# A transformer block with attention, feed-forward and experts: the identity products in TensorE's waits are taken out at the second feed-forward norm and in the router

## The chip, the cores and the metric

The kernel runs on one core of one Trainium2 chip. Its time is the device time of the launch in microseconds, the median of several runs. The engines are named as the profile names them: PE is TensorE's matmul, PEld its weight load, DVE is VectorE, ACT ScalarE, POOL GpSimd, SP SyncE, and a q behind a name is that engine's queue.

## The reference

The reference takes 256 tokens of 1024 features through three layers. All is float32. Cut to the calls that matter:

```python
def second_block(x, c, ...):
    for i in range(2):
        ...
        h = _modulate(x, sh_a, sc_a)          # rms norm, then * (1 + scale) + shift
        m = _neighborhood_attention(...) if i == 0 else _mla(...)
        x = x + g_a[:, None, :] * m
        h = _modulate(x, sh_f, sc_f)          # i == 0: the second feed-forward norm
        f = _swiglu(...) if i == 0 else _moe(h, w_router, w_gu, w_down)
        x = x + g_f[:, None, :] * f
    return _rmsnorm(x) * final_norm

def _moe(h, w_router, w_gu, w_down):
    ...
    probs = softmax(hf @ w_router)            # 8 experts
    vals, idx = lax.top_k(probs, 2)
    ...
    for e in range(8):
        y = y + combine[:, e:e + 1] * _swiglu(hf, w_gu[e], w_down[e])
```

Ahead of it, first_block is a layer of its own: norm, causal attention beside a recurrent unit, output projection, norm, feed-forward. So there are six norms that feed a projection, numbered 0 to 5 in the kernel: 0 and 1 in the first block, 2 and 3 in the first layer of the second, 4 and 5 in its last, where 5 is the one of the router.

## The kernel before

The 256 tokens stand in two row tiles of 128 (t = 0, 1), the features in eight column tiles of 128 (k). Weights come from HBM by SyncE's DMA queue into a ring of raw buffers. Most are split into a rounded high part (ScalarE, whi) and the rest (VectorE, wlo), and a product is then made of three: high by high, low by high, high by low. A raw buffer is loaded again when both parts are made, and the parts are made again when TensorE has used them. Each engine runs its own list in the order in which it is written, and semaphores tie them together.

The norm of stage s (whole_pair, L870, called by whole_columns) runs as follows. The output projection ahead of it ends row tile 0 first. VectorE multiplies it by its gate and adds it to x (L2172, L2173), ScalarE sums the squares (L1424), VectorE scales the rows by the reciprocal root (L1903). TensorE transposes the eight column tiles (L837) into PSUM, and ScalarE (k below 4, L1438) and VectorE (the others, L1908) modulate them into hx; for row tile 1 the two engines change sides. VectorE's list has the residual add of row tile 1 between the norm of row tile 0 and its modulation of it. TensorE multiplies two raw weight blocks by each tile of hx (whole_side, L859), turns row tile 1 in the middle of it, and ends with whole_rest (L867). In the stage of the second feed-forward norm (s = 3) the function fill makes two products of the 128x128 identity with 512 constant columns into a PSUM bank that is not used at that time, ahead of the first transposes. They end in no result.

The router (stage 5) works on both row tiles. TensorE transposes row tile 0 of x inside the last output projection (router_begin), makes its logits (L1267, eight columns), transposes row tile 1 (turn_rows, by halves as VectorE adds them up at L2375), and makes its logits. ScalarE copies the transposes (L1777), VectorE copies the last half (L2377). ScalarE sums the squares of row tile 1 behind its first copy. VectorE reads the logits (L2383), ranks them (L2395 to L2402) and names the two chosen experts of each token; five small products (L1281 to L1285) count places and totals; VectorE makes from the places the matrix that picks the rows of expert 0 (L2414), splits a weight block (L1893), and TensorE gathers these rows turned (L1299). VectorE modulates the first half of them (L2424), then works out from the totals which expert runs in which pass (L2442 to L2454, into eidi). SyncE, ScalarE and GpSimd wait for that list (sem experts_known); SyncE has by then filled all its buffers with the first weights of expert 0, and goes on with the next ones after it. The passes of the experts follow (expert_pass, L1341 and L1368). fill is called at five places in the router: one product after the logits of row tile 0, one after the transposes of row tile 1, two ahead of the wait for the chosen experts, one after the five small products, one after the gather.

Of the kernel before, what the change touches and what calls it, by code (L numbers as in the profile page):

```python
# [300 lines left out]
def blocks(nc, a, out):  # L301

    ctx = ExitStack()
    with ctx:
        base = [(nc.sbuf_base + LINE - 1) // LINE * LINE]

        def at(name, cols, dt=F32, offset=None, parts=P):

            if offset is None:
                offset = base[0]  # L310
                base[0] += (cols * 4 + LINE - 1) // LINE * LINE
                assert base[0] <= nc.sbuf_usable_end, (name, base[0], nc.sbuf_usable_end)
            t = nc.alloc_sbuf_tensor_at(name, [parts, cols], dt, offset=offset)
            return t.ap() if hasattr(t, "ap") and callable(t.ap) else t[:, :]
# [9 lines left out]
        def sem(name):  # L324
            if name not in sems:
                sems[name] = ctx.enter_context(nc.semaphore(name))
            return sems[name]
# [30 lines left out]
        cst = at("cst", C_ALL)  # L358
# [121 lines left out]
        ps = ctx.enter_context(nc.psum_tensor("ps", [P, 8, 512], F32))  # L480

        ident = cst[:, C_ID:C_ID + P]
# [12 lines left out]
        def vec(name):  # L495
            _, _, n, col = VEC[name]
            return vecs[:, col:col + n]
# [279 lines left out]
        def _(pe):  # L777
# [46 lines left out]
                        between()  # L824
                m.then_inc(mm_done, 2)

            def fill(bank, count):

                for _ in range(count):
                    pe.matmul(ps[:, bank, :], ident, cst[:, 0:512], start=True, stop=True)  # L830

            def turn_rows(rows_, s, t, by_half=None):

                for k in range(KT):
                    if by_half and k % 4 == 0:
                        pe.wait_ge(by_half, k // 4 + 1)
                    m = pe.transpose(ps[:, TURN_BANK[s] + 2 * t + k // 4, k % 4 * P:(k % 4 + 1) * P],  # L837
                                     rows_[:, t, k * P:(k + 1) * P], ident)
                    if k in (3, KT - 1):
                        m.then_inc(sem("turned"), 1)  # L840

            def turn(s, t):

                pe.wait_ge(sem("xn_ready"), XN0[s] + t + 1)
                turn_rows(xn, s, t)

            def whole_raw(c, width):

                ck = Chunk(c)
                pe.wait_ge(raw_in[ck.slot], 16 * ck.loads)  # L850
                return view(raws[ck.slot], KT, width)

            def whole_side(parts, t, s):

                for k in range(KT):
                    e, count = mods_until(s, t, k)
                    pe.wait_ge(mods_done[e], count)
                    for w, (o, cols) in parts:
                        pe.matmul(o[:, t * P:(t + 1) * P], w[:, k, cols], hx[:, t, k], start=(k == 0), stop=(k == KT - 1))  # L859
# [9 lines left out]

            def whole_pair(first, s, widths, pieces, after_turn=None, before_turn=None):  # L870

                fill(2, {1: 0, 3: 2}.get(s, 0))
                turn(s, 0)
                if after_turn:
                    after_turn()
                w = [whole_raw(first + i, widths[i]) for i in range(2)]
                whole_side([(w[i], pieces[i][0]) for i in range(2)], 0, s)
                if before_turn:
                    before_turn()
                turn(s, 1)  # L880
                for i in (1, 0):
                    whole_side([(w[i], pieces[i][1])], 0, s)
                return w
# [5 lines left out]
            def whole_columns(first, s, banks, after_turn=None):  # L889

                pieces = two_tiles(banks)
                w = whole_pair(first, s, (256, 256), pieces, after_turn)
                for i in range(2):
                    whole_rest(w[i], pieces[i], s)
# [297 lines left out]
            kv = [(ps[:, 5, 0:S], slice(0, KVL)), (ps[0:ROPE, 0, 0:S], slice(KVL, KVL + ROPE))]  # L1192
            queries = [(ps[:, 4, f * S:(f + 1) * S], slice(f * P, (f + 1) * P)) for f in range(2)]
            wd = whole_pair(W_MDN, 4, (KVL + ROPE, QL), (kv, queries), None, lambda: pe.wait_ge(sem("mod_read1"), 2))
            whole_rest(wd[0], kv, 4)
            latent_sum(0, (2,))
# [18 lines left out]
            for t in range(NT):  # L1215
                pe.wait_ge(sem("keys_read"), t + 1)
                tok = slice(t * P, (t + 1) * P)
                for lhs, rhs in ((lat_hi, h), (lat_hi, l), (lat_lo, h)):
                    for n in range(2):
                        m = pe.matmul(ps[:, 2 * t + n, :], lhs[:, 2, tok], rhs[:, n * 512:(n + 1) * 512],  # L1220
                                      start=(lhs is lat_hi and rhs is h), stop=(lhs is lat_lo))
# [36 lines left out]
            def logits(t):  # L1258

                for k in range(KT):  # L1260
                    if (t, k) == (1, 4):
                        pe.wait_ge(sem("x_half"), 3)
                    elif k % 4 == 0:
                        pe.wait_ge(sem("aT_ready"), AT0[5] + 2 * t + k // 4 + 1)
                    if (t, k) == (0, 0):
                        pe.wait_ge(sem("shift_read"), 1)
                    m = pe.matmul(ps[:, 4 + t, 0:NE], xT[:, t, k], rscaled[:, k], start=(k == 0), stop=(k == KT - 1))  # L1267
                m.then_inc(sem("logits"), 1)

            output_projection(W_MLO, KT, *mixes[3], 4, begun=2, last=(HEADS0[3] + H2) // 2, inside=router_begin)  # L1270
            logits(0)
            fill(0, 1)
            turn_rows(x, 5, 1, sem("x_half"))
            fill(0, 1)
            logits(1)

            fill(3, 2)
            pe.wait_ge(sem("chosen"), 1)
            sel = rw[:, 8:10, :].rearrange("p t e -> p (t e)")
            tri = cst[:, C_TRI:C_TRI + P]  # L1280
# [2 lines left out]
            pe.matmul(ps[:, 5, NE:2 * NE], ones, sel[:, 0:NE], start=False, stop=True).then_inc(sem("places"), 1)  # L1283
            pe.matmul(ps[:, 4, 0:NE], ones, sel[:, 0:NE], start=True, stop=False)
            pe.matmul(ps[:, 4, 0:NE], ones, sel[:, NE:2 * NE], start=False, stop=True).then_inc(sem("totals"), 1)  # L1285
            fill(3, 1)

            def begin_expert(c, p):
                ck = ExpertChunk(c, p, PASS_CHUNKS)
# [3 lines left out]
            def gather_turned():  # L1293

                pe.wait_ge(sem("pick_ready"), 1)
                pe.wait_ge(sem("xn_ready"), XN0[5] + NT)
                for k in range(KT):
                    for t in range(NT):
                        m = pe.matmul(ps[:, 6 + k // 4, k % 4 * P:(k % 4 + 1) * P], xn[:, t, k * P:(k + 1) * P],  # L1299
                                      pick[:, t, :].bitcast(F32), start=(t == 0), stop=(t == NT - 1))  # L1300
                    if k == 3:
                        m.then_inc(sem("gathered_first"), 1)
                m.then_inc(sem("gathered_turned"), 1)
# [12 lines left out]
                m.then_inc(sem("ge_turned"), 1)  # L1316

            gather_turned()
            fill(0, 1)

            def expert_pass(p, last):

# [62 lines left out]
            for n in range(2):  # L1385
                pe.wait_ge(sem("last_ready"), n + 1)
                for t in range(NT):
                    for d in (dchi, dclo):
                        m = pe.matmul(ps[:, 6 * (1 - t) + n, :], pickT[:, t * P:(t + 1) * P], d[:, n * 512:(n + 1) * 512],
                                      start=(d is dchi), stop=(d is dclo))  # L1390
# [5 lines left out]
        def _(act):  # L1396
# [79 lines left out]
            for name, (tile, row, count, _) in VEC.items():  # L1476
                if name not in SP_ROWS:
                    ld(rows[row:row + count, tile, :], VEC_SRC[name](a), "rows_in")
# [1219 lines left out]
```

## Time and profile before

| | |
|---|---|
| time, median of three runs | 1258.85 us |
| the three runs | 1258.27, 1258.85, 1261.66 us |
| span of the profiled execution (the page gives no other time of it) | 1258.0 us |
| TensorE busy | 1224.1 us, 97% of the span |
| VectorE busy | 1016.2 us, 81% |
| ScalarE busy | 779.0 us, 62% |
| TensorE's mean granted clock | 0.996 of full speed |
| HBM read and written | 375.4 MB, 298 GB/s over the span |

The span is that of one execution under the profiler, and all positions and durations below are from it. A busy TensorE is not one at its peak: the page counts an instruction as busy from its start to its modelled end, and neighbouring matmuls overlap. So the duration of a group is read off the chain of waits, where each piece ends where the next begins. A float32 product stands in the trace as two instructions, a transpose and a product of the rounded parts as one.

### The profile page before, as it was taken

How to read it: one execution, taken by the hardware profiler on the slowest of the kernel's cores; microseconds unless marked ns; L12 is line 12 of the kernel's file. 1: busy time of each engine (PE TensorE's matmuls, PEld its weight loads, DVE VectorE, ACT ScalarE, POOL GpSimd, SP SyncE). 2: the span in 40 equal slices, each digit the busy share in tenths (PEclk: the TensorE clock that was granted, in tenths of full speed). 3: DMA queues.
4: the chain of work that ended last, by engine and by line, in shares of the span. 5: the costliest groups of instructions: out<-in, count | busy, mean ns of one | idle time of the engine just before them, and what ended most of it. 6: DMA issues, size and time to landing. Idle time of an engine off the chain costs nothing.

```text
span 1258.0 us, 20244 instructions
## 1 busy us (share of the span) xinstructions
PE 1224.1 (97%) x7668; PEld 1086.8 (86%) x7668; DVE 1016.2 (81%) x1095; ACT 779.0 (62%) x992; POOL 93.1 (7%) x111
## 2 busy tenths in 40 slices
PE   9989999999999999999999999999999999999995
PEld 7978999987998799998897777898989898989884
DVE  6797899996756588777756578989898989898987
ACT  5765666644655455443346556777777777777764
POOL 0020000000562100000002202000000000000020
PEclk9999999999999999999999999999999999999998
DMA  9953997679944569998973239999999999999991
GB/s 322 377 200 102 337 314 270 246 289 252 250 159 162 181 215 325 332 349 308 382 253 97 79 140 394 379 406 355 401 351 409 348 408 349 408 345 411 347 410 73
DMA packets 163981, 369.08 MB, mean 293 GB/s; under 512 B 24420, under 2 KB 96559, under 8 KB 157511
## 3 DMA queue, kind: packets, MB, share of 16 engines
q1 hardware_dynamic: 157345, 350.72, 78.0%
q10 hardware_dynamic: 5094, 12.11, 2.5%
q0 software_dynamic: 1472, 5.28, 1.1%
q8 instruction: 49, 0.80, 0.3%
q14 instruction: 21, 0.17, 0.0%
HBM read 360.72 MB, written 14.70 MB: 298 GB/s over the span
## 4 chain that ended last, share of the span: by engine, by line
PE 71%; DVE 12%; ACT 4%; issue 4%; DMA 3%; SPq 3%; POOL 2%; ACTq 0%; DVEq 0%
PE ps L1341 20%; PE ps L795 7%; PE ps L797 7%; PE ps L796 7%; PE ps L1368 6%; PE ps L807 4%; PE ps L809 4%; PE ps L811 4%; DVE wlo L1893 3%; SPq L712 2%; PE ps L859 2%; PE ps L867 2%; DMA raw<-in_moe_w_gu 2%; DVE third_lo L1893 2%; DVE wlo L1885 1%
## 5 line engine op out<-in xcount | busy, mean ns | idle before, releaser
L1406 ACT ACTIVATE whi<-raw 128x1024 fp32r<-128x1024 f32 x186 | 192.6, 1057 | 152.0 <-PE ps L797 96.1
L1885 DVE TENSOR_TENSOR wlo<-raw,whi 128x1024 fp32r<-128x1024 f32 x186 | 227.1, 1248 | 72.8 <-ACT whi L1406 69.3
L795 PE MATMUL ps<-ahi,whi 128*128 128x256 f32 x832 | 234.3, 282 | 0.3 <-ACT qT L1591 0.3
L796 PE MATMUL ps<-alo,whi 128*128 128x256 f32 x832 | 231.8, 279 | 0.0
L797 PE MATMUL ps<-ahi,wlo 128*128 128x256 f32 x832 | 231.8, 279 | 0.0
L1893 DVE TENSOR_TENSOR wlo<-raw,whi 128x1792 fp32r<-128x1792 f32 (+1 forms) x96 | 199.3, 2089 | 24.4 <-ACT whi L1420 24.3
L1420 ACT ACTIVATE whi<-raw 128x1792 fp32r<-128x1792 f32 (+1 forms) x96 | 167.5, 1758 | 55.9 <-PE ps L1368 24.0
L795 PEld LDWEIGHTS ps<-ahi,whi 128*128 128x128 f32 x832 | 156.9, 189 | 1.7 <-issue 0.8
L796 PEld LDWEIGHTS ps<-alo,whi 128*128 128x128 f32 x832 | 156.7, 188 | 0.7 <-issue 0.7
L797 PEld LDWEIGHTS ps<-ahi,wlo 128*128 128x128 f32 x832 | 156.9, 189 | 0.0
L1341 PE MATMUL ps<-whi,hchi 128*128 128x448 f32 x352 | 101.8, 370 | 4.0 <-DVE wlo L1893 2.7
L1341 PE MATMUL ps<-wlo,hchi 128*128 128x448 f32 x352 | 99.1, 362 | 0.0
L1341 PE MATMUL ps<-whi,hclo 128*128 128x448 f32 x352 | 99.0, 362 | 0.0
L1341 PEld LDWEIGHTS ps<-whi,hchi 128*128 128x128 f32 x352 | 63.8, 187 | 16.5 <-DVE wlo L1893 6.7
L1893 DVE TENSOR_TENSOR third_lo<-raw,third_hi 128x1792 fp32r<-128x1792 f32 (+1 forms) x32 | 66.8, 2088 | 10.8 <-ACT third_hi L1420 10.7
L1420 ACT ACTIVATE third_hi<-ada 128x1792 fp32r<-128x1792 f32 (+2 forms) x32 | 51.2, 1601 | 31.4 <-PE ps L1341 18.9
L1341 PEld LDWEIGHTS ps<-wlo,hchi 128*128 128x128 f32 x352 | 66.0, 188 | 4.5
L1341 PEld LDWEIGHTS ps<-whi,hclo 128*128 128x128 f32 x352 | 66.0, 188 | 4.6
L1893 DVE TENSOR_TENSOR third_lo<-ada,third_hi 128x1792 fp32r<-128x1792 f32 (+2 forms) x32 | 60.3, 1886 | 7.4 <-ACT third_hi L1420 7.4
L1893 DVE TENSOR_TENSOR wlo<-ada,whi 128x1792 fp32r<-128x1792 f32 (+2 forms) x32 | 60.4, 1887 | 4.5 <-ACT whi L1420 4.3
L2611 POOL TENSOR_SCALAR probs<-probs,small 128x256 f32<-128x256 f32 (+1 forms) x80 | 48.7, 623 | 187.0 <-DVE small L2025 186.7
L1420 ACT ACTIVATE whi<-ada 128x1792 fp32r<-128x1792 f32 (+2 forms) x32 | 51.0, 1595 | 17.4 <-PE ps L1341 16.0
(350 smaller groups left out, 2431.7 us busy)
## 6 DMA issues: line engine op xcount, KB each, us to landing
raw<-in_moe_w_gu SPq DMA_DIRECT2D x96, 896.0 KB, 7.0
ada<-in_w_ada SPq DMA_DIRECT2D x48, 1024.0 KB, 7.4
raw<-in_moe_w_down SPq DMA_DIRECT2D x32, 1024.0 KB, 7.9
ada<-in_moe_w_gu SPq DMA_DIRECT2D x32, 896.0 KB, 7.3
raw<-in_w_up SPq DMA_DIRECT2D x22, 1024.0 KB, 5.8
raw<-in_ffn_w_gu SPq DMA_DIRECT2D x22, 1024.0 KB, 9.1
ada<-in_moe_w_down SPq DMA_DIRECT2D x16, 1024.0 KB, 9.2
raw<-in_na_w_qkv SPq DMA_DIRECT2D x12, 1024.0 KB, 8.4
```

What stands on the lines that cost most here:

```text
L795: pe.matmul(o, h[:, k, cols], bhi[:, k], start=(k == 0), stop=False)
L796: pe.matmul(o, h[:, k, cols], blo[:, k], start=False, stop=False)
L797: m = pe.matmul(o, l[:, k, cols], bhi[:, k], start=False, stop=(k == KT - 1))
L807: pe.matmul(o, bhi[at_k][:, tok], h[:, k, n0:n0 + n], start=first, stop=False)
L809: pe.matmul(o, bhi[at_k][:, tok], l[:, k, n0:n0 + n], start=False, stop=False)
L811: m = pe.matmul(o, blo[at_k][:, tok], h[:, k, n0:n0 + n], start=False, stop=last)
L1341: m = pe.matmul(ps[:, 2 * part + n, 0:EC], lhs[:, kk], rhs[:, k, n * EC:(n + 1) * EC], start=(kk == 0 and lhs is hchi and rhs is h), stop= ...
L1368: m = pe.matmul(ps[:, 4 + n, :], lhs[:, k0 + k], rhs[:, k, n * 512:(n + 1) * 512], start=(k0 + k == 0 and rhs is h and lhs is gchi), stop= ...
L1406: act.activation(high_, src, ACT.Copy).then_inc(hi_done, 1)
L1420: act.activation(high_[:, 0:k * n], raws[ck.slot][:, 0:k * n], ACT.Copy).then_inc(moe_hi, 1)
L1885: ve.tensor_tensor(low_, src, high_.bitcast(F32), ALU.subtract).then_inc(lo_done, 1)
L1893: ve.tensor_tensor(low_[:, 0:k * n], raws[ck.slot][:, 0:k * n], high_[:, 0:k * n].bitcast(F32), ALU.subtract)\
```

## The change

Every call of fill goes, and the function with them. Nothing is put in their place, and no semaphore changes.

```diff
-            def fill(bank, count):
-
-                for _ in range(count):
-                    pe.matmul(ps[:, bank, :], ident, cst[:, 0:512], start=True, stop=True)
-
...
             def whole_pair(first, s, widths, pieces, after_turn=None, before_turn=None):
 
-                fill(2, {1: 0, 3: 2}.get(s, 0))
                 turn(s, 0)
...
             logits(0)
-            fill(0, 1)
             turn_rows(x, 5, 1, sem("x_half"))
-            fill(0, 1)
             logits(1)
 
-            fill(3, 2)
             pe.wait_ge(sem("chosen"), 1)
...
             pe.matmul(ps[:, 4, 0:NE], ones, sel[:, NE:2 * NE], start=False, stop=True).then_inc(sem("totals"), 1)
-            fill(3, 1)
...
             gather_turned()
-            fill(0, 1)
```

## Rows read from the trace of the kernel before

**Rows 1.** Waits of TensorE, 445 to 735 us: total, times, longest (us).
```profile
PE ps L984 <- DVE alo L2030: 0.3, 1, 0.3
```

**Rows 2.** Timeline of SyncE's queue: start, length, DMA issues of a line.
```profile
748.69 5.77 SPq L644 DMA_DIRECT2D raw<-in_moe_w_gu  x4
```

**Rows 3.** Windows: length, busy time of each engine (count), PEclk, DMA share, GB/s.
```profile
59.00:62.00 3.00, 3.00 (x28) 3.00 (x27) 1.97 (x6) 3.00 (x10) 0.00 (x0) 1.00 0.99 404
66.50:69.50 3.00, 3.00 (x16) 3.00 (x15) 3.00 (x3) 2.98 (x5) 0.00 (x0) 0.50 0.02 5
309.50:310.70 1.20, 0.10 (x2) 0.08 (x1) 0.47 (x2) 1.17 (x5) 0.00 (x0) 1.00 0.90 132
...
745.60:746.80 1.20, 0.00 (x0) 0.00 (x0) 1.03 (x7) 1.17 (x4) 0.00 (x0) 1.00 0.00 0
...
770.00:780.00 10.00, 8.77 (x43) 7.47 (x41) 6.88 (x5) 4.40 (x3) 0.00 (x0) 1.00 1.03 415
```

**Rows 4.** Chain of waits at the second feed-forward norm: start, length (us).
```profile
440.11 1.72 PE ps L830 x4
...
442.90 3.81 PE ps L859 x32
446.71 0.87 PE ps L837 x8
```

**Rows 5.** Timeline of VectorE and ScalarE at the same norm.
```profile
441.41 1.23 DVE L2173 TENSOR_TENSOR x<-x,xn 128x1024 f32<-128x1024 f32 x1
442.30 1.51 ACT L1438 ACTIVATE hx<-ps,mod 128x128 f32<-128x128 f32 x4 [3.71 <-PE ps L837]
442.74 1.37 DVE L1908 TENSOR_SCALAR hx<-ps,mod 128x128 f32<-128x128 f32 x4
443.69 1.07 ACT L1424 ACTIVATE xn<-x 128x1024 f32<-128x1024 f32 x1
445.40 0.76 DVE L1903 TENSOR_SCALAR xn<-x,small 128x1024 f32<-128x1024 f32 x1
```

**Rows 6.** Chain of waits in the router.
```profile
730.75 1.68 PE ps L1267 x16
732.44 0.96 PE ps L830 x2
...
733.87 0.60 ACT xT L1777
734.47 1.05 ACT xn L1424 x2
...
736.74 0.36 DVE rw L2383 x2
...
738.93 0.39 PE ps L1281 x2
...
740.21 0.96 PE ps L830 x2
741.17 1.80 PE ps L1299 x16
```

**Rows 7.** Timeline of VectorE and TensorE in the router.
```profile
731.52 0.69 DVE L2375 TENSOR_TENSOR x<-x,xn 128x512 f32<-128x512 f32 x1
...
732.85 0.69 DVE L2375 TENSOR_TENSOR x<-x,xn 128x512 f32<-128x512 f32 x1
...
734.31 0.69 DVE L2377 COPY xT<-ps 128x512 f32<-128x512 f32 x1 [0.77 <-PE ps L837]
...
736.67 1.96 PE L830 MATMUL ps<-cst 128*128 128x512 f32 x4
...
740.29 0.48 DVE L2414 TENSOR_SCALAR pick<-cst,posn 128x128 fp32r<-128x128 f32 x2
740.69 2.02 DVE L1893 TENSOR_TENSOR wlo<-raw,whi 128x1792 fp32r<-128x1792 f32 x1
```

**Rows 8.** Timeline of TensorE ahead of the fall of its clock.
```profile
65.96 0.78 PE L998 MATMUL ps<-cst,probs 128*128 128x128 f32 x3 [1.55 <-POOL probs L2611]
```

## The prediction

> **What bounds the kernel now.** I read TensorE's own waits first, then SyncE and the windows behind the router, then the chain of waits and the timeline around each place where the change cuts, and at last the windows that give the granted clock. Between the second feed-forward norm and the router TensorE hardly waits: the longest wait there is 0.3 us [rows 1]. A microsecond won on TensorE at the norm is therefore a microsecond won until the router. In the router the chain changes engine with every step (TensorE, ScalarE, VectorE and back), so there a product counts only where the next step waits for it. After the router the chain passes from VectorE's list of experts to SyncE, which takes up the expert weights again at 748.69 [rows 2]; from then on the DMA engines are full, a share of 1.03 and 415 GB/s between 770 and 780 us [rows 3]. What moves that list moves the end.
>
> **What is taken out.** Each call of fill makes products of the identity with 512 columns; a product is two instructions in the trace. Four instructions are 1.72 us on the chain [rows 4], so one product is 0.86 us. Eight products go: two ahead of the norm's first transposes, six in the router. The call for the first feed-forward norm had count 0, so nothing changes there. No wait and no transfer is added or moved, and no other engine loses an instruction.
>
> **The norm: 1.45 us earlier.** The two products are on the chain from 440.11 to 441.83, and the transposes of the first row tile follow them [rows 4]. That tile has long been ready, so without them the transposes start at 440.11. Not all of the 1.72 us stays, because VectorE becomes late. The eight modulated tiles are shared: ScalarE makes the first four, VectorE the last four, and VectorE starts its four only after the residual add of the second row tile, 441.41 + 1.23 = 442.64 [rows 5]. It starts them at 442.74 with or without the products. TensorE reaches the fifth tile after half of its 3.81 us [rows 4]: 442.90 - 1.72 + 1.9 = 443.08. The tile is there at 442.74 + 1.37/4 = 443.08 and a hand-over later, so at most 0.1 to 0.2 us is lost. More is lost at the second transposes. They need the second normalised row tile, ready at 445.40 + 0.76 = 446.16 now [rows 5]. Its squares on ScalarE (443.69) wait today behind ScalarE's own four tiles; without the products those (1.51 us from 440.11 + 0.47 on, [rows 5]) are done by 442.1, and the squares start when x is complete, at about 442.72. That is 0.97 us earlier, so the row tile is ready at 445.19 and the transposes start at about 445.25 instead of 446.71 [rows 4]: 1.46 us. I take 1.45. Bounds: 1.72 if VectorE's hand-overs were free, 0 if something after it does not move.
>
> **The router: 1.05 us earlier at full clock.** (a) The product ahead of the second transposes and the one after them. The product stands at 732.44 to 733.40 on the chain [rows 6]. The first half of x is there at 731.52 + 0.69 = 732.21 [rows 7], so the four transposes of it move 0.96 us forward, ScalarE's copy of them (0.60 us, now at 733.87) ends at about 733.5, and the squares of the second row tile, now at 734.47, wait instead for x itself, 732.85 + 0.69 = 733.54 [rows 6, 7]. They gain 0.8 to 0.9 us; I take 0.8. The other branch, the logits, must arrive as early: last transposes at 733.56 plus 0.45, VectorE's copy 0.69 (today it begins at 734.31, [rows 7]), then eight instructions of 1.68/16 = 0.105 us [rows 6], about 735.6. Now VectorE reads the logits at 736.74 [rows 6]; minus 0.8 that is 735.94, so the logits are not late. (b) The two products at 736.67, 1.7 us on the chain's measure, run while VectorE ranks the logits; TensorE's next real product starts at 738.93 on VectorE's result [rows 6, 7]. They cost nothing now and gain nothing. (c) The product at 740.21 keeps the gather until 741.17 [rows 6], though the pick matrix is there at 740.29 + 0.48 = 740.77 [rows 7]: 0.4 us less a start of 0.1 to 0.15, so 0.25. What is late next is VectorE's 2.02 us split at 740.69 [rows 7], which stands ahead of its reading of the gather: moved by 0.8 it ends at 741.9, and the first half of the gather (1.80 us, [rows 6]) ends at 739.97 + 0.06 + 1.80 = 741.85 instead of 742.97. So 0.8 + 0.25 = 1.05 us. (d) The last product lies before a wait: TensorE does nothing from 745.6 to 746.8 [rows 3]. Gain nothing. Together with the norm, 2.5 us.
>
> **What the products covered: the clock.** The trace has one place where the granted clock fell in mid-kernel. TensorE stood idle for 1.55 us before 65.96, after a few short attention products [rows 8]; from 66.50 to 69.50 the rows show 0.50, the 1.2 GHz level, and TensorE got through 16 instructions where it had got through 28 in the 3 us from 59 to 62 [rows 3]: a factor of 1.75. At the third norm, 1.1 us of idle in 309.50 to 310.70 left the clock at 1.00 [rows 3]. At the norm that is changed the new idle pieces are 0.2 and 0.35 us, shorter than the one that left the clock alone, so I cost it at nothing there. In the router it is another matter. After the change TensorE ends the logits at about 735.6, stands until 738.1, runs ten instructions of 8 columns (738.93 to 740.21 today, [rows 6]), stands until 740.0 and then gathers: over 4 us with 1.28 us of light work, thinner than what stood ahead of the fall at 66. I take a fall there as likely. Its price by the rows: three microseconds at half clock do the work of 3/1.75 = 1.7, so 1.3 us if all of it is on the path. If it starts at 738.1 it slows the six rank products ahead of the pick (0.77 us by 0.58) and the first part of the gather by some 0.3, together 0.9; if it starts in the pause before the gather it takes 1.3. I take 1.2; bounds 0 and, for a stretch twice as long, 2.6. Sum: -1.45 - 1.05 + 1.2 = -1.3 us.
>
> The Trainium skill, in "TensorE: Matmul & The Clock Gate", section "Part 1: The HAM clock gate", has it that half rate is the default and that activity lifts it. By that rule the fillers buy speed and the sum is -1.3; by the row at 309.50 they buy nothing and the sum is -2.5.
>
> **The rivals.** One: the clock holds in the router, as it held at 309.50 [rows 3]. Against it stands the thin work from 735.6 to 740.0. Time: -2.5 us. Two, on the other side: the clock stays low from the second tile's logits through the gather and the experts' first products. Place: TensorE, 734 to 750 us. Price at 0.75 of the time of each step on the path: last transposes and logits (0.45 + 0.84) 0.95, rank products 0.58, first half of the gather 1.35, and up to 1.3 for the first expert products; together 4.2, so +1.7 us. It turns the sign from 2.5 us on; the first three make 2.9 by themselves. For it: the logits have 8 columns an instruction, and the last cover, before 746.8, goes as well. Against it: the logits' weight loads keep TensorE going, and delays of the first expert products lie beside a DMA stream that is full [rows 3]. The Trainium skill, in "TensorE: Matmul & The Clock Gate", section "HAM oscillation — how this bites in real kernels", describes such a case, short bursts between waits that start at half rate each time; no stretch of this trace shows it twice in a row. Three: the norm's gain does not reach the end, because a weight load or a split keeps its time. Against it: TensorE waits for nothing over 0.3 us until 735 [rows 1], and loads are issued when splits free their buffers, so they move along. Time: -1.05 + 1.2 = +0.15 us.
>
> **How the numbers follow.** The profiled span is 1258.0 us, 0.85 below the median of the three runs, 1258.85; the page gives no other time of that execution. The differences are carried to the median. Forecast (one fall): 1258.85 - 1.3 = 1257.55, chance 0.5. No fall: 1256.35, 0.2. Low clock throughout: 1260.55, 0.17. Gain lost at the norm: 1259.0, 0.13. The runs of one kernel lie 0.6 below to 2.8 above their median, which is more than some of these differences; I go from 0.75 below the second case to 0.75 above the third: 1255.6 to 1261.2. A measurement of this kernel can tell about 0.3%, 3.8 us, from no change; none of the four cases reaches that, and only a sum of a case with the spread of the runs does: faster 0.06, same 0.84, slower 0.10.
>
> **What would show it.** Right: the transposes of the norm follow the projection at once, and TensorE's first modulated product runs some 1.7 us, the second transposes 1.45 us earlier than now, relative to the end of the projection; the rank products start 0.8 us earlier relative to the first logits; the granted clock is below 1.00 somewhere in the 10 us around the gather; SyncE takes up the expert weights about 1.3 us earlier in all. Wrong: a granted clock under 1.00 at the norm, a clock of 1.00 all through the router, a new wait of TensorE between norm and router, or an expert pass whose length changes from its period now.

## The result, and the profile after

The changed kernel took 1264.03 us (median of four runs, 1263.14 to 1265.63) beside 1259.59 us of the kernel before in the same measurement: a ratio of 1.0039, 95% interval [1.0025, 1.0053]. It is slower by 0.39%, where the prediction said 1257.6 us and no measurable change. Later measurements of the same two kernels came out smaller, 1.0013 [0.9995, 1.0032] and 1.0027 [1.0013, 1.0041]. Over everything measured the mean of the changed kernel is 1263.17 us (28 runs) and that of the kernel before 1260.33 us (190 runs): 2.84 us more, plus or minus 0.96 (95%), or 0.22%. One run of the kernel before, 2037.76 us at a mean granted clock of 0.556, was in a slow state and is left out. The loss is real; the first measurement probably shows it too large. The measurements behind the first ran on three chips, and the mean of the kernel before lay between 1259.7 and 1261.3 us in them, so comparisons across measurements are less sharp than their intervals say.

The head of the page of the changed kernel:

```profile
span 1261.3 us, 20212 instructions
PE 1220.9 (97%) x7652; PEld 1088.0 (86%) x7652; DVE 1018.7 (81%) x1095; ACT 778.8 (62%) x992; POOL 90.5 (7%) x111
```

TensorE is busy for less time than before (1220.9 us, 1224.1 before) and the span is 3.3 us longer. Cut into stages by rows of the timeline, the two profiled executions differ so:

| stage | before | after | difference |
|---|---|---|---|
| start, to the last product of the projection ahead of the norm | 439.48 | 442.42 | +2.9 |
| norm: from there to the second transposes | 7.07 | 5.71 | -1.36 |
| from there to the last product of the last projection | 283.58 | 283.59 | 0.0 |
| router: from there to the list of experts | 16.44 | 18.70 | +2.26 |
| from the list to the end | 511.43 | 510.88 | -0.55 |

So 0.9 us of the 3.3 arose where the change was made. The 2.9 us lie ahead of any edit, and a section below tells what they are.

**The norm went as worked out.** The chain of waits in the changed kernel, at the norm (start, length, what; a line of the code has another number in each kernel, so the transposes are L837 before and L832 here):

```profile
442.58 0.48 PE ps L811 x2
...
443.09 1.24 DVE xn L2161
...
444.35 1.24 DVE x L2162
...
447.32 0.77 DVE xn L1892
...
448.13 1.09 PE ps L832 x8
449.22 3.57 PE ps L854 x32
```

The chain leaves TensorE at the end of the projection and runs over VectorE's residual add (444.35) and second row tile (447.32) to the second transposes at 448.13. Before, it ran over the products and TensorE's own work [rows 4]. VectorE has become the bound, which is why 1.36 of the 1.72 us stay.

**The router lost its clock.** The chain there:

```profile
735.84 2.67 PE ps L1261 x16
738.53 0.24 DVE rw L2372
...
740.60 0.60 PE ps L1272 x2
741.20 0.43 PE ps L1273 x2
...
743.12 3.69 PE ps L1289 x16
746.84 1.37 DVE hc L2413 x4
```

The logits of the second tile (L1261) took 2.67 us; before, the chain ran over those of the first tile, the same sixteen instructions, in 1.68. The first two instructions of the rank products (the five small ones that count places and totals; L1272, 0.60) took 0.39, and the first half of the gather (L1289, 3.69) took 1.80 [rows 6]. On TensorE's timeline the gather began at 741.01 in the kernel before:

```profile
741.01 3.73 PE L1299 MATMUL ps<-pick,xn 128*128 128x128 f32 x32
```

so up to 742.97, where its first half ended on the chain, it took 1.96 us; the chain counts 1.80 because the gather overlaps the product ahead of it. Windows of the changed kernel (length, busy time of PE, PEld, DVE, ACT, POOL with counts, PEclk, DMA share, GB/s):

```profile
735.50:736.00 0.50, 0.50 (x8) 0.50 (x5) 0.12 (x1) 0.50 (x1) 0.00 (x0) 1.00 0.00 0
736.00:736.50 0.50, 0.50 (x6) 0.50 (x5) 0.50 (x1) 0.47 (x3) 0.00 (x0) 0.83 0.00 0
...
740.00:743.00 3.00, 2.30 (x10) 2.21 (x10) 1.24 (x8) 0.03 (x1) 0.00 (x0) 0.50 0.00 0
743.00:746.50 3.50, 3.38 (x16) 3.38 (x17) 2.00 (x2) 0.00 (x0) 0.00 (x0) 0.50 0.00 0
...
746.50:747.00 0.50, 0.50 (x6) 0.50 (x6) 0.16 (x1) 0.00 (x0) 0.00 (x0) 0.93 0.00 0
```

TensorE's timeline shows where the logits lie, and the wait behind them in brackets:

```profile
735.68 2.82 PE L1261 MATMUL ps<-rscaled,xT 128*128 128x8 f32 x16
740.60 0.60 PE L1272 MATMUL ps<-rw,cst 128*128 128x8 f32 x2 [2.10 <-DVE rw L2391]
```

The granted clock falls to 0.50 within the logits (736.0 to 736.5) and comes back at about 746.5, within the gather: 10.2 us at the 1.2 GHz level. The kernel before had 1.00 throughout this stretch. SyncE takes up the expert weights at 752.54, where it did at 748.69 [rows 2]:

```profile
752.54 5.76 SPq L644 DMA_DIRECT2D raw<-in_moe_w_gu  x4
```

Of these 3.85 us, 2.9 are from the start, -1.36 from the norm, 2.26 from the router.

This is not a matter of one trace. The granted clock as a mean over a whole run is 0.990 to 0.993 in all 28 runs of the changed kernel. In the 186 runs of the kernel before whose clock is on record it is 0.993 to 0.998, and 0.993 in only three of them.

### The profile page after: what moved, and what is told of

It is laid out like the page before. It is cut to its first block, busy times and chain, and to the rows that moved or that the text cites. A ratio compares the mean times of both kernels' runs of the same rounds, so it can differ in the third digit from the quotient of the medians.

```text
span 1261.3 us, 20212 instructions
## 1 busy us (share of the span) xinstructions
PE 1220.9 (97%) x7652; PEld 1088.0 (86%) x7652; DVE 1018.7 (81%) x1095; ACT 778.8 (62%) x992; POOL 90.5 (7%) x111
## 4 chain that ended last, share of the span: by engine, by line
PE 78%; DVE 11%; ACT 4%; issue 4%; DMA 1%; POOL 1%; ACTq 0%; DVEq 0%; SPq 0%
PE ps L1330 22%; PE ps L797 7%; PE ps L796 7%; PE ps L795 7%; PE ps L1357 6%; PE ps L807 5%; PE ps L809 5%; PE ps L811 5%; PE ps L862 3%; DVE wlo L1882 3%; PE ps L854 2%; DVE third_lo L1882 2%; DVE wlo L1874 1%; PE ps L992 1%; DMA expert_in<-xn,sendi 1%
## 5 line engine op out<-in xcount | busy, mean ns | idle before, releaser
L1409 ACT ACTIVATE third_hi<-raw 128x1792 fp32r<-128x1792 f32 (+1 forms) x32 | 56.1, 1752 | 7.3 <-PE ps L1330 5.8
```

Of the source, the lines that this page charges most:

```text
L1409: act.activation(high_[:, 0:k * n], raws[ck.slot][:, 0:k * n], ACT.Copy).then_inc(moe_hi, 1)
```

## The experiments

Stages are cut as in the table above. "Pace" is the time from one product to the next in the gate and up products of the second feed-forward, which lie in the stage between norm and router (there are 960 of these products). Differences of times are means against the runs of the kernel before in the same measurement, with 95%.

### Norm alone, router alone, and both kernels again

r1_norm_only:

```diff
-                fill(2, {1: 0, 3: 2}.get(s, 0))
```

> Only the two products ahead of the second feed-forward norm's first transposes go; the router keeps its six. Theory A (the loss of the change arises in the router, from a granted clock that stays at 1.2 GHz for 10.24 us there): this kernel is 1.3 us faster than before, the row of the second transposes comes 1.33 us earlier after the end of the projection, the router's clock stays at 1.00. Theory B (the loss is not of the change: TensorE waits 2.47 instead of 0.57 us at 327 us, ahead of everything that was changed, and its clock falls there): the time is 1.3 us faster or up to 1.7 us slower by whether that wait appears, and the trace shows which.

r2_router_only takes out the router's five calls alone.

> Only the six products of the router go; the norm keeps its two. Theory A: 1.7 to 2.3 us slower than before, with the clock at 0.50 for about 10 us between the second tile's logits and the end of the gather; the gather's first half takes about 3.7 instead of 1.80 us. Theory B: within 1 us of before in a run without the long wait at 327 us, some 3 us slower with it.

r3_after_again is the changed kernel, r4_before_itself the kernel before as a kernel of its own.

> The changed kernel once more. In its first trace the change itself explains +0.36 us (norm -1.33, router +2.24, experts -0.55) and the 2.96 us ahead of the norm are left. Theory A, if the first measurement stands: again 3 to 6 us slower than before. Theory B: the difference shrinks towards +0.4 us, and a trace without the long wait at 327 us has a span near 1258.4 us.

> The kernel before against itself. Theory A: ratio 1.000 with an interval of about 0.1%, and its trace shows the wait at 327 us as short as the first one did, 0.6 us. Theory B: the runs spread over 3 us, and a share of the traces has the long wait at 327 us although nothing is changed.

| run | norm | norm to router | router | list to end | ratio | difference, us |
|---|---|---|---|---|---|---|
| r1_norm_only | 5.70 | 287.89 | 16.44 | 510.51 | 0.9984 [0.9966, 1.0002] | -1.2 ± 1.6 |
| r2_router_only | 7.07 | 283.57 | 19.14 | 514.19 | 1.0019 [1.0000, 1.0038] | +3.7 ± 2.0 |
| r3_after_again | 5.71 | 283.62 | 19.33 | 512.10 | 1.0013 [0.9995, 1.0032] | +2.3 ± 1.5 |
| r4_before_itself | 7.07 | 283.56 | 16.44 | 508.79 | 0.9984 [0.9964, 1.0004] | -1.4 ± 1.7 |

The parts act alone as they do together: the norm's cut is worth 1.37 us at the norm and leaves the router at 16.44; the router's cut costs 2.7 us there and leaves the norm at 7.07. r4 shows what a time can tell: the kernel before lies 1.4 us from itself, within its interval. Windows of r2_router_only, with the low clock from the logits on, as in the changed kernel but longer (13.7 us):

```profile
734.00:737.00 3.00, 2.67 (x17) 2.67 (x17) 2.02 (x5) 2.96 (x5) 0.00 (x0) 0.68 0.00 0
737.00:740.00 3.00, 0.99 (x5) 0.90 (x5) 1.79 (x8) 2.15 (x4) 0.00 (x0) 0.50 0.00 0
```

r1 holds a surprise: the stage behind the norm is 4.3 us longer, with the clock at 1.00. That is taken up below.

### Which products held the clock

r5_off_path_kept takes out those on the path (both around turn_rows and the one before the pick) and the norm's, and keeps those that the chain of waits never touched, the two behind the second logits and the one behind the gather. r6_covers_out does the reverse.

```diff
             logits(1)
-            fill(3, 2)
...
             gather_turned()
-            fill(0, 1)
```

(r6_covers_out.) r8_last_cover_only is the changed kernel with the product behind the gather put back.

> Out: the two products of the norm and the three of the router that the chain ran through (ahead of and behind the second tile's transposes, ahead of the gather). Kept: the two behind the second tile's logits and the one behind the gather, which lay in waits. Stage lengths of the trace: from the last product of the last attention projection to the list of experts 16.44 us in before, 18.70, 19.14 and 19.33 where all six were out. Theory A (the clock stays low for 10 us and more because all that TensorE does between the second logits and the gather is thin, and thin work at half clock does not lift it): two products in that stretch end the low clock early or prevent it: 15.4 to 17 us, low clock at most 3.4 us there. Theory B (one pause is enough, and then the clock takes its 10 us whatever follows): 18.5 us or more, low clock 10 us.

> Out: the two products behind the second tile's logits and the one behind the gather, which were not on the chain. Kept: the norm's two and the router's three on the chain. Theory A: the pause behind the logits (735 to 739 in before's positions) lets the clock fall once, and the product ahead of the gather with the gather itself lifts it: 16.4 to 18 us from the last projection product to the list of experts. Theory B: 18.5 us or more with 10 us of low clock. If these three products covered nothing: 16.44 us, clock 1.00.

> The changed kernel with one product put back, the one behind the gather. It separates what the missing cover costs behind the list of experts (511.43 and 508.79 us in the two traces of before, 510.88, 512.10 and 514.19 where the router's products were out) from what is chance. Theory A: the router is as long as in the changed kernel, 18.7 to 19.4 us, since the low clock is made ahead of the gather; the stretch behind it stays within 508.8 to 511.5 us. Theory B (the last product covers the experts' first weights, and without it the first pass is longer): the stretch behind the list is shorter here than in the changed kernel by 1 to 2 us.

| run | router, us | low clock in it, us | difference, us |
|---|---|---|---|
| kernel before | 16.44 | none | |
| r6_covers_out | 18.10 | 3.4 | +0.8 ± 1.2 |
| r5_off_path_kept | 18.47 | 10.2 | +3.9 ± 2.1 |
| r8_last_cover_only | 18.80 | 10.2 | +3.5 ± 1.6 |
| changed kernel, three traces | 18.70, 19.33, 18.70 | 10.2, 13.7, 10.2 | |

TensorE's timeline of r5_off_path_kept (start, length, what, in brackets the idle time before it), then three of its windows:

```profile
731.21 0.66 PE L837 MATMUL ps<-cst,x 128*128 128x128 f32 x4 [0.66 <-DVE x L2371]
731.70 2.01 PE L1266 MATMUL ps<-rscaled,xT 128*128 128x8 f32 x16
733.56 3.12 PE L830 MATMUL ps<-cst 128*128 128x512 f32 x4
...
738.83 6.51 PE L1295 MATMUL ps<-pick,xn 128*128 128x128 f32 x32 [0.22 <-DVE pick L2410]
```

```profile
731.00:734.00 3.00, 2.79 (x21) 2.55 (x22) 2.08 (x6) 2.96 (x5) 0.00 (x0) 1.00 0.00 0
734.00:737.00 3.00, 3.00 (x8) 1.34 (x6) 1.61 (x7) 2.03 (x4) 0.00 (x0) 0.54 0.00 0
737.00:740.00 3.00, 2.78 (x13) 2.69 (x14) 2.06 (x5) 0.00 (x0) 0.00 (x0) 0.50 0.00 0
```

The two kept products came too late. The clock fell just after they began (at about 734.2 us), they themselves took 3.12 us (1.96 before [rows 7]) and now stood in the way. That the pause behind the logits alone takes the clock, and that a product in it holds it, is refuted: TensorE had no pause there, and the clock was low for 10.2 us. What stood ahead of the fall is the thin work of the transposes and 8-column logits with 0.66 us of idle between them. Not every run of r5 went this way: the mean granted clock is 0.990 to 0.993 in eight of its ten runs, but 0.995 and 0.996 in two. By the stages of its trace r5 should be 0.7 us slower than before (router +2.0, norm -1.4); of its +3.9 ± 2.1 us the rest is not traced. r6 shows the other half (TensorE's timeline, then two windows):

```profile
735.64 1.02 PE L830 MATMUL ps<-cst 128*128 128x512 f32 x2
736.50 1.85 PE L1267 MATMUL ps<-rscaled,xT 128*128 128x8 f32 x16
740.45 0.39 PE L1280 MATMUL ps<-rw,cst 128*128 128x8 f32 x2 [2.11 <-DVE rw L2400]
...
741.59 2.02 PE L830 MATMUL ps<-cst 128*128 128x512 f32 x2
743.40 4.53 PE L1298 MATMUL ps<-pick,xn 128*128 128x128 f32 x32
```

```profile
740.00:743.00 3.00, 2.55 (x12) 1.92 (x13) 1.89 (x7) 0.74 (x3) 0.00 (x0) 0.77 0.00 0
743.00:746.00 3.00, 3.00 (x18) 2.60 (x17) 1.24 (x1) 0.00 (x0) 0.00 (x0) 0.66 0.03 5
```

With the products around the transposes in place the logits ran at full speed (1.85 us). The clock fell after the pause of 2.11 us, when the rank products (0.39 for the first two instructions, as before) were through: the product ahead of the gather (2.02 us) and the gather's first half paid for it. So products of no cost by the chain, which I had priced at nothing, are worth 1.66 us. In these two traces each group guarded what came behind it, and neither guarded the whole alone.

### Products only where TensorE waits

If the products hold the clock and those on the path cost 1 us, both gains should be had by moving them. r7_moved (the norm's call is out as well):

```diff
-            def fill(bank, count):
+            def fill(bank, count, n=512):
...
-                    pe.matmul(ps[:, bank, :], ident, cst[:, 0:512], start=True, stop=True)
+                    pe.matmul(ps[:, bank, 0:n], ident, cst[:, 0:n], start=True, stop=True)
...
                 for k in range(KT):
+                    if by_half and k == 4:
+                        fill(0, 1)
...
             logits(0)
-            fill(0, 1)
             turn_rows(x, 5, 1, sem("x_half"))
-            fill(0, 1)
             logits(1)
...
-            fill(3, 1)
+            fill(3, 1, 256)
...
             gather_turned()
-            fill(0, 1)
+            fill(0, 2)
```

> The norm's two products are out; the router's stand in waits alone: one between the two halves of the second tile's transposes, two behind the logits, a half one (256 columns) ahead of the gather, two behind the gather. Theory A: no low clock in the router, 15.4 us from the last projection product to the list of experts instead of 16.44, the norm 1.36 us shorter, so about 2.4 us faster than before in the mean of many runs. Theory B: a pause is left here and there, the clock falls, 18 us or more and no faster than before.

TensorE's timeline of r7_moved, and two windows:

```profile
730.67 0.63 PE L839 MATMUL ps<-cst,x 128*128 128x128 f32 x4
731.14 1.02 PE L830 MATMUL ps<-cst 128*128 128x512 f32 x2
732.00 0.62 PE L839 MATMUL ps<-cst,x 128*128 128x128 f32 x4
732.46 2.01 PE L1268 MATMUL ps<-rscaled,xT 128*128 128x8 f32 x16
734.32 1.96 PE L830 MATMUL ps<-cst 128*128 128x512 f32 x4
```

```profile
734.00:737.00 3.00, 2.71 (x13) 1.41 (x12) 2.34 (x10) 2.78 (x4) 0.00 (x0) 1.00 0.00 0
737.00:740.00 3.00, 2.91 (x23) 2.51 (x23) 2.41 (x5) 0.00 (x0) 0.00 (x0) 1.00 0.03 5
```

One product now lies between the two halves of the transposes, where TensorE stood for 0.66 us in r5, and the clock stays at 1.00. In the router, ahead of the place where the clock fell in r5, the two kernels differ in this product alone; the clock stayed at 1.00 there in all eight traces that have it (r7, r9, r13 to r18). The router takes 15.63 us: 0.81 less than before and 3.1 less than the changed kernel's 18.70. The time did not follow, though: 1261.35 us, +1.1 ± 1.3 against before. By the stages it should have been 2.2 us faster.

### Where the norm's gain goes

r9_moved_norm_kept is r7 with the norm's two products back; r10_norm_only_again, r11_after_again2 and r12_before_again repeat.

> The router's products stand in the waits as in the moved version, but the norm keeps its two products. In the moved version the trace was 2.2 us shorter than before by its stages, yet the mean of 13 runs was 1.1 us longer than that of 35 runs of before. In the second feed-forward's gate and up products two paces were seen, 0.113 and 0.118 us for each product over the whole stage, 283.6 and 287.9 us from the second transposes to the last projection product; the slow one in two of six traces without the norm's products and in none of four with them. Theory C (without the norm's products the slow pace is the more frequent one): this kernel has the fast pace, 283.6 us, a router of 15.6 us, and its mean is about 0.8 us below before. Theory D (the pace is chance, alike in both): the pace may be either, the mean again lies near that of the moved version.

> Only the norm's products out, once more. Theory C: more than half of the runs lie some 4 us above the lowest ones, the mean is 0 to 1.5 us above before's, the trace has the slow pace of 0.118 us (287.9 us from the second transposes to the last projection product) more likely than not. Theory D: the mean is 1.36 us below before, the trace has the fast pace, as in eight of ten traces so far.

> The changed kernel for the third time. By stages: norm -1.36, router +2.3 to +2.9, so +0.9 to +1.5 us at the same pace. Theory C: +0.9 to +1.5 and a further 4.3 us in the runs with the slow pace, +2.5 to +4.5 us in the mean. Theory D: +0.9 to +1.5 us in the mean.

> The kernel before once more, for its pace. Theory C: the fast pace (283.6 us from the second transposes to the last projection product), router 16.44 us. Theory D: either pace.

r10 had again 287.88 us between norm and router, 4.3 more than r9, r11 and r12 (283.54, 283.61, 283.54), and its runs fell into two groups, five at 1257.4 to 1259.9 us and seven at 1261.1 to 1264.6. Those of r9 make one group, 1256.35 to 1260.90. Groups of run times alone do not tell the stage, though: the kernel before itself, as r4, has eight runs at 1257.0 to 1259.9 and four at 1262.1 to 1263.9. The extra time in the trace is spread over the whole stage. TensorE's timeline at the same place, in the kernel before and then in r1:

```profile
479.80 0.28 PE L797 MATMUL ps<-ahi,wlo 128*128 128x256 f32 x1
479.91 0.28 PE L795 MATMUL ps<-ahi,whi 128*128 128x256 f32 x1
...
480.93 0.28 PE L795 MATMUL ps<-ahi,whi 128*128 128x256 f32 x1
```

```profile
479.83 0.28 PE L795 MATMUL ps<-ahi,whi 128*128 128x256 f32 x1
479.95 0.28 PE L796 MATMUL ps<-alo,whi 128*128 128x256 f32 x1
...
480.89 0.28 PE L795 MATMUL ps<-ahi,whi 128*128 128x256 f32 x1
```

From the first to the last row it is ten products in 1.13 us in the one, 0.113 us each, and nine in 1.06 us in the other, 0.118 each. The instruction is the same, no wait stands between, and the granted clock is 1.00 in both. A trace keeps one of the two paces through that stage, 283.6 or 287.9 us (288.1 in r17), and none lies between; 960 products at 0.0045 us more make the 4.3 us. The slow pace is nothing new: in the kernel before, the same lines of the first feed-forward, whose norm has no product, ran at it, ten products in 1.18 us:

```profile
199.95 0.28 PE L795 MATMUL ps<-ahi,whi 128*128 128x256 f32 x1
...
201.13 0.28 PE L796 MATMUL ps<-alo,whi 128*128 128x256 f32 x1
```

Nor is it fixed by the code. That first feed-forward and all ahead of it are the same in every kernel here, and 17 of the 20 traces ran it at 0.118 throughout, while r5, r14 and r15 began it at 0.113 and went over to 0.118 between 209 and 217 us (r15 ran at 0.113 again for some 5 us after that).

r13_both_moved and r15_both_moved_again put a short product into the wait that the norm's cut had left (the second transposes begin 4.00 us behind the first products in the changed kernel, 3.65 before), r14_moved_again and r16_moved_norm_kept_again repeat r7 and r9; r17_ahead_of_gate_up puts it ahead of the gate and up products, and r18_one_at_norm keeps one of the norm's two.

```diff
+                if s == 3:
+                    fill(2, 1, 128)
                 turn(s, 1)
```

(r13, r15, besides r7's edits.)

```diff
             def gate_up(gu, stage):
+                if stage == 3:
+                    fill(2, 1, 128)
```

(r17.)

```diff
-                fill(2, {1: 0, 3: 2}.get(s, 0))
+                fill(2, {1: 0, 3: 1}.get(s, 0))
```

(r18.)

> The router's products stand in its waits (as in r9), the norm's two products are out, and one short product (128 columns, 0.2 us) stands in the wait of 0.3 us ahead of the second transposes. Theory C1 (the slow pace of 0.118 us comes from TensorE's pause there): pace 0.113, 283.6 us from the second transposes to the last projection product, mean 2.2 us below before. Theory C2 (the slow pace has another origin and comes in a share of the executions without the norm's products): the pace is slow in the trace with a chance of some 40%, and the mean is 0.5 us below before or above it.

> The moved version without any product at the norm, again. Theory C (the slow pace is frequent without the norm's products): mean at or above before's although router and norm are 2.2 us shorter by their stages; the slow pace in the trace with a chance of a half or more. Theory D (chance): 2.2 us below before.

> As r13, for a second trace. Theory C1: pace 0.113. Theory C2: slow with a chance of some 40%.

> The router's products in its waits, the norm's two kept, again. Theory C: pace 0.113 (as in six of six such traces), router 15.6 us, mean 0.8 us below before. Theory D: either pace, and the mean anywhere from 0.8 below to 1 us above.

> The router's products in its waits, no product at the norm, one short product (128 columns, 0.2 us) directly ahead of the gate and up products. Theory E (the pace is set at the entry of the stage, and another instruction there sets it anew): the runs are no longer in two groups, pace 0.113 always, mean 2 us below before. Theory C2 (it is set by how TensorE passes the norm): two groups some 4 us apart, some 40% in the upper one, mean about 0.5 us below before.

> The router's products in its waits, one product at the norm in place of two. Stages: norm about 0.7 us shorter than before, router 0.8. Theory C2: one group of runs, pace 0.113, mean 1.5 us below before. Theory E: two groups some 4 us apart, as without any product at the norm.

| at the norm | traces at 0.113 | traces at 0.118 |
|---|---|---|
| two products (before, r2, r4, r6, r9, r12, r16) | 7 | 0 |
| none (after, r1, r3, r5, r7, r8, r10, r11, r14) | 6 | 3 |
| a short one in the wait (r13, r15) | 0 | 2 |
| a short one ahead of gate and up (r17) | 0 | 1 |
| one (r18) | 0 | 1 |

The theory that the idle 0.35 us before the second transposes brings the slow pace falls with r13 and r15: that wait was filled and both traces were slow. That a product right ahead of the stage's products would set the fast pace falls with r17. r18 gives up 0.5 us of the gain (norm 6.21) and is slow as well. What sets the pace stays open; shown is only that it differs and that no trace with both products at the norm had the slow one. Seven traces are few, and that the products keep the slow pace away is not shown. They are not needed for the fast one either: 6 of 9 traces have it without. The price fits the times: 3 slow traces in 9 make 1.4 us on average (an estimate from these nine traces; the pace of the other runs was not traced), which is the norm's 1.36 us. Norm alone, r1 and r10 together, is +0.2 ± 1.0 us against all runs of before.

The moved products, in all runs of each kernel against the mean of before: with the norm's two kept (r9, r16) -1.3 ± 0.8 us at 1259.03; with none there (r7, r14) -0.6 ± 1.1; with the short one (r13, r15) -1.5 ± 1.2. Against the runs of before in the same measurements these are -0.9 ± 0.8, 0.0 ± 1.0 and -1.1 ± 1.2, and r7 and r14, one and the same kernel, lie at +1.1 ± 1.3 and -1.9 ± 1.6. The first is the soundest, since its gain is about that of one stage, the router's 0.8 us. None is a gain of more than 0.12% against all runs, and by the ratios within one measurement none can be told from no change (r9 0.9994 [0.9984, 1.0003], r13 and r14 0.9989 [0.9974, 1.0003]); by the means r9 (-1.2 ± 0.9) and r14 just can. The rest: r12 +0.9 ± 1.3, r11 +2.7 ± 1.8, r17 +1.5 ± 1.5, r18 +0.9 ± 1.1.

### The 2.9 us ahead of the change

VectorE, GpSimd and TensorE in the changed kernel, ahead of the second attention block (timeline):

```profile
318.63 6.56 DVE L1932 TENSOR_TENSOR alo<-hx,ahi 128x512 fp32r<-128x512 f32 x4 [1.12 <-ACT ahi L1459]
318.31 14.69 POOL L2608 TENSOR_TENSOR bias2a<-bias2a,cst 128x512 f32<-128x512 f32 x8 [226.85 <-DMA bias2a<-in_na_rpb]
329.73 0.36 PE L807 MATMUL ps<-whi,ahi 128*128 128x256 f32 x1 [2.47 <-issue]
```

and in the kernel before:

```profile
318.68 4.66 DVE L1943 TENSOR_TENSOR alo<-hx,ahi 128x512 fp32r<-128x512 f32 x4 [1.13 <-ACT ahi L1470]
319.73 14.92 POOL L2619 TENSOR_TENSOR bias2a<-bias2a,cst 128x512 f32<-128x512 f32 x8 [228.22 <-DMA bias2a<-in_na_rpb]
327.88 0.36 PE L807 MATMUL ps<-whi,ahi 128*128 128x256 f32 x1 [0.57 <-issue]
```

GpSimd got its DMA 1.4 us sooner and began with VectorE's four instructions; these took 6.56 us for 4.66, TensorE stood 2.47 us for 0.57, and its clock was 0.52 on average from 330.0 to 333.5, where it was 1.00 before. The two go together in five traces: VectorE's four instructions took 6.56, 6.56, 6.26, 5.74 and 4.66 us in the changed kernel, r10, r12, r4 and the kernel before, and TensorE stood 2.47, 2.47, 2.16, 1.64 and 0.57 us, each time 4.1 us less. r10 and r12, the second of them the kernel before itself, show the same fall of the clock at the same place: it is chance, and not the change.

## Why the prediction was wrong

**The norm: right.** 1.36 us against 1.45, and by the reason given, VectorE's residual add. The clock stayed at 1.00 there.

**What follows the norm: missed.** The bound "0 if something after it does not move" was in the text, and rival three named a weight load or a split that keeps its time. Neither happened (TensorE's waits in the changed kernel are 0.7 us at the longest up to 738 us). What ate the gain, in some traces, was the pace of the gate and up products behind it. The trace of before held a sign of it, 0.118 us a product in the first feed-forward against 0.113 in the second, and I had not compared them; the page's mean of one product is its duration, 0.28 us in both.

**The router at full clock: right, a little high.** In r7 the clock held and the path was free. Counted from the last product of the projection, VectorE read the logits 0.80 us sooner than before (0.8 in step (a)), the gather began 0.91 sooner (1.05 with step (c)), and the list came 0.81 sooner.

**(b) and (d), "they cost nothing now and gain nothing": wrong.** r6 took out just these three and the router grew by 1.66 us. The text had said that the products hold the clock, but it priced this in one sum for all eight, and costed the three off the path at nothing.

**The price of the clock: the step that failed.** "I take 1.2" rested on one stretch of 3 us, begun at the rank products or in the pause behind them. The clock was low for 10.2 to 13.7 us, from within the second tile's logits into the gather. The steps that rival two named were the right ones. Counted from the last product of the projection, the changed kernel begins the second logits 0.88 us sooner (735.68 - 731.72 against 734.97 - 730.13), the rank products 0.08 later, the pick matrix 0.70 later, the gather 0.52 later, and VectorE reads it 2.25 later. So the logits cost 0.99 us on the chain (0.95 in rival two, with the transposes), the rank products 0.62 (0.58), the gather's first half 1.73 (1.35); the start of the gather won 0.18 back, step (c). Only the last term, up to 1.3 us for the first expert products, did not come: the clock was back at 746.5. The factor of 1.75, taken from counts of instructions in two windows of 256-column products, was a little small: the gather's first half went from 1.96 to 3.69, a factor of 1.9, and a rank instruction pair on the chain from 0.22 to 0.43. The stage is 2.26 to 2.89 us longer in three traces, and with the full-clock gain of 0.8, taken over from r7, the price is 3.1 to 3.7, above the bound of 2.6 for the case I took as likeliest. With 1.36 at the norm the two edited places lose 0.9 to 1.5 us; rival two had +1.7, the forecast -1.3. The evidence against rival two, that no stretch stood twice in a row in this trace, came from one fall that was followed by a dense stream of 256-column products; it said nothing of a fall into 8-column products and pauses. The section "HAM oscillation — how this bites in real kernels" of the Trainium skill ("TensorE: Matmul & The Clock Gate") describes short bursts of products, each followed by a wait of 3 to 5 us for DMA, after which the next burst runs at half rate. The trace agrees in part: the granted clock was 0.50 through short work between waits, but it fell within the logits (736.0 to 736.5), when the longest wait of the stretch had been 0.66 us and the one of 2.10 us was still to come.

**The sum: carried to a weak base.** 1258.85 us, the median of three runs, lies 1.5 us under the mean of 190 runs of the same kernel (1256.6 to 1266.8). Rival two's 1260.55 on that base is 1262.0 on the mean; the measured mean is 1263.2. Of the first measurement's 4.4 us, 0.9 to 1.5 are the edited places and 1.4 what the slow pace costs on average; the rest is not traced in those runs; the later measurements are smaller (+2.3 and +2.7 us). The upper end of the range, 0.75 above rival two's 1260.55, should read 1261.3 and not 1261.2.

**The delay behind the router passes through.** From the second expert pass on the period is 61.05 to 61.11 us in every trace, and the stage from the list to the end lies between 508.6 and 514.2 us in all of them. It is not shorter where the list was late: its mean is 511.3 us in the six traces whose clock was low for 10 us or more in the router and 509.9 in the other fourteen, and the longest, r2's, holds one more fall of the clock (0.50 from 786.3 to 789.7). So nothing shows that the full DMA stream swallowed the delay, as rival two's counterargument had it.

## What to carry to other kernels

A filler product that the chain of waits never touches is not thereby free to go: look at what follows it, and count the clock's price on each of these steps, up to the row where the granted clock is back. To keep the clock at no cost, put small products into TensorE's waits ahead of thin work, not behind it, and see in the granted clock that they came in time. And before a gain of 1 us is believed, repeat the kernel before: its own runs here lie 10 us apart, and a gain at one stage was undone, in some traces, by another pace of the next.

## What the runs showed of the hardware that was not expected

- Once down, the clock can stay down through work that leaves TensorE nearly busy: r5 shows 10.2 us at 0.50 with no wait above 0.3 us in it, the 512-column products among them. In r6, where one such product and the gather followed the fall, it was back after 3.4 us.
- One and the same stream of 256-column products runs at 0.113 or 0.118 us a product at a granted clock of 1.00, for a whole stage, 4.3 us in all; in r5, r14 and r15 it changed from the one to the other within a stage.
- GpSimd's 128x512 additions beside VectorE's subtractions of that size slow these: four took 6.56 us where they took 4.66 when GpSimd began 1.4 us later, and 3.59 in r11, where GpSimd began 1.3 us behind the first of them.
